# A transformer kernel on one Trainium2 core: suffix sums and strict mask of the stick-breaking heads as f32r products, the logs split in two parts

## What is computed

```
z = q k^T * scale
log_keep = where(s < t, -softplus(z), 0)
tail = cumsum(log_keep from the last key back) - log_keep
w = where(s < t, exp(log_sigmoid(z) + tail), 0)
out = w v
```

## Time and profile before

| | |
|---|---|
| median of 3 runs | 2950.47 us (2950.24 to 2952.39) |
| profiled execution, own time | 2949.88 us |
| its span | 2948.1 us, 34780 instructions |
| PE busy | 2692.4 us (91%) |
| PEld busy | 2109.6 us (72%) |
| DVE busy | 1543.8 us (52%) |
| ACT busy | 967.8 us (33%) |
| POOL busy | 333.3 us (11%) |
| mean DMA | 119 GB/s |

### The profile page before, as it was taken

One profiled execution on the slowest core, in us unless ns is written; L12 is line 12 of the kernel. 1 busy time (PEld: TensorE's weight loads), 2 busy tenths in 40 slices (PEclk: granted clock), 3 DMA queues, 4 the chain that ended last, 5 costly groups with the idle time before them and its releaser, 6 DMA issues. The chain is left out here.

```text
span 2948.1 us, 34780 instructions
## 1 busy us (share of the span) xinstructions
PE 2692.4 (91%) x14205; PEld 2109.6 (72%) x14205; DVE 1543.8 (52%) x2162; ACT 967.8 (33%) x1349; POOL 333.3 (11%) x193
## 2 busy tenths in 40 slices
PE   6899999999998999999998898999997788997975
PEld 5777688888876777888886787888775755685542
DVE  4672356544637523555544763565645488455413
ACT  3243433222322534322222332333531178430001
POOL 0000004422400000044421000000100000001110
PEclk8999999999989999999999998999998799898998
DMA  4211124443412111244443132233423120148996
GB/s 130 70 60 44 58 86 129 132 142 117 122 59 69 58 43 55 91 140 137 135 129 100 57 91 80 96 91 103 129 77 130 61 87 2 60 168 320 418 419 273
DMA packets 274792, 351.27 MB, mean 119 GB/s; under 512 B 55108, under 2 KB 251972, under 8 KB 261956
## 3 DMA queue, kind: packets, MB, share of 16 engines
q1 hardware_dynamic: 266084, 327.97, 33.1%
q0 software_dynamic: 8448, 20.98, 2.0%
q10 hardware_dynamic: 96, 0.02, 0.0%
HBM read 332.13 MB, written 25.17 MB: 121 GB/s over the span
## 5 line engine op out<-in xcount | busy, mean ns | idle before, releaser
L199 PE MATMUL ps<-h_hi,w_hi 128*128 128x512 f32 x1760 | 709.4, 403 | 60.4 <-DVE room L823 21.3
L200 PE MATMUL ps<-h_lo,w_hi 128*128 128x512 f32 x1760 | 695.6, 395 | 0.0
L201 PE MATMUL ps<-h_hi,w_lo 128*128 128x512 f32 x1760 | 695.6, 395 | 0.0
L176 ACT ACTIVATE w_hi<-w_raw 128x2048 fp32r<-128x2048 f32 (+1 forms) x170 | 322.3, 1896 | 875.2 <-PE ps L201 867.1
L181 DVE TENSOR_TENSOR w_lo<-w_raw,w_hi 128x2048 fp32r<-128x2048 f32 (+1 forms) x170 | 435.9, 2564 | 253.6 <-ACT w_hi L176 253.6
L199 PEld LDWEIGHTS ps<-h_hi,w_hi 128*128 128x128 f32 x1760 | 337.6, 192 | 144.7 <-issue 72.5
L201 PEld LDWEIGHTS ps<-h_hi,w_lo 128*128 128x128 f32 x1760 | 336.3, 191 | 72.6
L200 PEld LDWEIGHTS ps<-h_lo,w_hi 128*128 128x128 f32 x1760 | 337.6, 192 | 70.1 <-issue 1.9
L201 PE MATMUL ps<-merged_hi,w_lo 128*128 128x512 f32 x640 | 252.8, 395 | 0.0
L199 PE MATMUL ps<-merged_hi,w_hi 128*128 128x512 f32 x640 | 252.8, 395 | 0.0
L200 PE MATMUL ps<-merged_lo,w_hi 128*128 128x512 f32 x640 | 252.8, 395 | 0.0
(11 more groups left out here) (456 smaller groups left out, 3767.9 us busy)
## 6 DMA issues: line engine op xcount, KB each, us to landing
w_raw<-in_w_in SPq DMA_DIRECT2D x284, 256.0 KB, 3.7
w_raw<-in_w_up SPq DMA_DIRECT2D x128, 256.0 KB, 3.6
w_raw<-in_w_down SPq DMA_DIRECT2D x128, 256.0 KB, 3.6
room<-in_w_ada SPq DMA_DIRECT2D x96, 256.0 KB, 5.9
expert_over_h<-in_w_exp_down SPq DMA_DIRECT2D x10, 1024.0 KB, 26.0
w_raw<-in_w_out SPq DMA_DIRECT2D x32, 256.0 KB, 3.5
spilled<-projected POOLq DMA_DIRECT2D x32, 256.0 KB, 2.5
w_raw<-in_w_ssm_out SPq DMA_DIRECT2D x32, 256.0 KB, 3.6
```

Source lines behind the costliest of these rows:

```text
L176: act.activation(self.hi[:, q, :, 0:cols], raw[:, q, :, 0:cols], ACT.Copy).then_inc(self.hi_ready, 1)
L199: pe.matmul(out, w[0], x[0], start=start, stop=False)
L200: pe.matmul(out, w[0], x[1], start=False, stop=False)
L201: return pe.matmul(out, w[1], x[0], start=False, stop=stop)
```

## The change

The suffix sums and the mask become f32r matmuls. The four constants (identity, strict mask, triangle, all ones) are rounded once at the start of each layer by ACT. The output of `softplus` is rounded by ACT (`split_high`) and the remainder taken by DVE (`split_low`); each of the 10 products of a head is made twice, with the high and with the low part. `suffix_sums` waits for `sp_low`, `logs(h)` of the next pair waits for `sp_low` in place of `r_ready`, and the wait for `ob_ready` moves from `weights` to `split_high`. The buffers of the stage are laid out anew: the two parts take the place of `room_w`, `swa_p` and `swv`, and `w` is in the room of the high part.

```diff
+            ident_r, strict_r, suffix_r, ones_r = (in_halves(n, [P, P]) for n in ("ident_r", "strict_r", "neg_suffix_r", "neg_ones_r"))
...
+            sp_hi, sp_lo = in_halves("sp_hi", [P, 2, PACK]), in_halves("sp_lo", [P, 2, PACK])
...
                 def scores(i):
                     if i == 0:
+                        pe.wait_ge(rounded, 4)
...
-                            mm = pe.matmul(z_ps(h)[:, SOFF[b]:SOFF[b] + P], self.c("ident"), self.c("strict"), start=False, stop=True, skip_group_check=True)
+                            mm = pe.matmul(z_ps(h)[:, SOFF[b]:SOFF[b] + P], ident_r[:], strict_r[:], start=False, stop=True, skip_group_check=True)
...
                 def suffix_sums(h):
-                    pe.wait_ge(sp_ready, h + 1)
+                    pe.wait_ge(sp_low, h + 1)
                     for b in range(TB):
                         for j in range(b, TB):
                             a = SOFF[b] + P * (j - b)
-                            mm = pe.matmul(z_ps(h)[:, a:a + STRIP[j]], self.c("neg_suffix") if j == b else self.c("neg_ones"),
-                                           sp_[:, h % 2, SOFF[j]:SOFF[j] + STRIP[j]], start=False, stop=j == TB - 1, skip_group_check=True)
+                            for part in (sp_hi, sp_lo):
+                                mm = pe.matmul(z_ps(h)[:, a:a + STRIP[j]], suffix_r[:] if j == b else ones_r[:], part[:, h % 2, SOFF[j]:SOFF[j] + STRIP[j]],
+                                               start=False, stop=j == TB - 1, skip_group_check=True)
                     mm.then_inc(r_ready, 1)
...
                 def logs(h):
                     act.wait_ge(z_ready, h + 1)
                     if h >= 2:
-                        act.wait_ge(r_ready, h - 1)
+                        act.wait_ge(sp_low, h - 1)
...
+                def split_high(h):
+                    act.wait_ge(sp_ready, h + 1)
+                    if h >= 2:
+                        act.wait_ge(ob_ready, h // 2)
+                    act.activation(sp_hi[:, h % 2], sp_[:, h % 2], ACT.Copy).then_inc(sp_high, 1)
+
                 def weights(h):
                     act.wait_ge(r_ready, h + 1)
-                    if h >= 2:
-                        act.wait_ge(ob_ready, h // 2)
...
+                for to, name in ((ident_r, "ident"), (strict_r, "strict"), (suffix_r, "neg_suffix"), (ones_r, "neg_ones")):
+                    act.activation(to[:], self.c(name), ACT.Copy).then_inc(rounded, 1)
...
                 logs(0)
                 logs(1)
                 for i in range(SBH // 2):
+                    split_high(2 * i)
+                    split_high(2 * i + 1)
                     if i >= 1:
                         take_values(i - 1)
...
+                def split_low(h):
+                    dve.wait_ge(sp_high, h + 1)
+                    dve.tensor_tensor(sp_lo[:, h % 2], sp_[:, h % 2], sp_hi[:, h % 2].bitcast(F32), ALU.subtract).then_inc(sp_low, 1)
...
                 softplus(0)
                 softplus(1)
                 for i in range(SBH // 2):
+                    split_low(2 * i)
+                    split_low(2 * i + 1)
                     for t in beside(i):
                         dense(t)
```

More of the change, by code:

```diff
@@ L493, in mix @@
                 "z_ready", "absd", "z_expd", "logd", "sp_ready", "r_ready", "w_ready", "ob_ready", "ob_taken"))
-            room = sb("mix_room", [P, 4 * PACK])
-            swv, v = sb("swv", [P, TB, SWK]), sb("v", [P, TB, SBW])
-            p = sb("swa_p", [P, 2, TB, BAND])
+            sp_high, sp_low, rounded = sem("sp_high"), sem("sp_low"), sem("rounded")
+            v = sb("v", [P, TB, SBW])
             mx, neg, den, sink, inv = (sb(f"swa_{x}", [P, 2, TB]) for x in ("mx", "neg", "den", "sink", "inv"))
@@ L499, in mix @@
             x_rs, t_rs = sb("x_rs", [P, S]), sb("token_rs", [P, TB])
-            part = lambda a, n: room[:, a * S:(a + n) * S].rearrange("p (n s) -> p n s", s=S)
-            sq, rs, tc, ts = part(0, 2), part(2, 4), part(6, 2), part(8, 2)
+            in_halves = lambda n, shape: st.enter_context(nc.sbuf_tensor(f"{n}_{l}", shape, F32R))
+            ident_r, strict_r, suffix_r, ones_r = (in_halves(n, [P, P]) for n in ("ident_r", "strict_r", "neg_suffix_r", "neg_ones_r"))
+            until_band = st.enter_context(ExitStack())
+            at_first = lambda n, shape: until_band.enter_context(nc.sbuf_tensor(f"{n}_{l}", shape, F32))
+            room = sb("mix_room", [P, 2 * PACK])
+            room_w, p, swv = at_first("mix_room_w", [P, 2 * PACK]), at_first("swa_p", [P, 2, TB, BAND]), at_first("swv", [P, TB, SWK])
+            until_band.close()
+            sp_hi, sp_lo = in_halves("sp_hi", [P, 2, PACK]), in_halves("sp_lo", [P, 2, PACK])
+            chunks_of = lambda a, n: a.rearrange("p (n s) -> p n s", s=S)[:, 0:n]
+            tc = chunks_of(room_w[:, 0:4 * S], 4)[:, 0:2]
+            rs, sq = chunks_of(room[:, 0:4 * S], 4), chunks_of(room_w[:, 2 * S:4 * S], 2)
+            ts = p[:].rearrange("p i b n -> p (i b n)").rearrange("p (n s) -> p n s", s=S)[:, 0:2]
             pt = room[:, 0:2 * len(turns) * P].rearrange("p (i n) -> p i n", i=2)
-            sp_, w = (room[:, i * 2 * PACK:(i + 1) * 2 * PACK].rearrange("p (i n) -> p i n", i=2) for i in range(2))
+            sp_, w = (a[:].rearrange("p (i n) -> p i n", i=2) for a in (room, room_w))
             x = self.swq
```

## The result

The changed kernel took 2957.86 us (median of 10 runs, 2953.98 to 2962.26), the kernel before in the same session 2951.10 (10 runs, 2949.36 to 2953.45): a ratio of 1.0021, with a 95% interval from 1.0012 to 1.0031. It is 6.8 us slower; the prediction called a change slower from 0.2% on, and the interval has this bound inside it, so the two are not told apart. The profiled execution took 2956.63 us with a span of 2954.8, against 2949.88 and 2948.1 before.

What follows compares the result with a forecast made beforehand. The PE, never idle in the stick-breaking stage, was taken as the bound. Pairs -7.2, short-stall clock falls +5.1 and first-pair falls +4.4 gave +2.3 us: about 2952.5 us for the median, range 2944 to 2960.

Steps and rivals of the forecast that it cites:

- The PE's saving: Stick-breaking stage: suffix sums 2.76 us a head against 4.25, mask 0.90 us a pair; 32 us if nothing else changed.
- The chain from z to the suffix sums: ACT and DVE list orders delay a pair's first suffix sums until 11.23 us after its first mask matmul.
- The stalls: New PE waits on `split_low` before suffix sums: 4.8 us in two first pairs, 2.4 in six others.
- A pair: Two heads in the stage: 30.45 us, against 29.47 in 2 pairs and 31.97 in 6; -7.2 us in all.
- The clock: PE clock falls after stalls: 3 of 6 short ones, +5.1 us; both first pairs at 2.2 us each, +4.4.
- The stages in all: Both layers' stick-breaking stages together: -7.2 + 5.1 + 4.4 = +2.3 us.
- Rival (a): The clock holds in the short stalls: -2.8 us, 2947.7; chance 0.20.
- rival (b): The clock falls in every pair, and for longer: 2957 to 2965 us, slower; chance 0.16.
- (c): No stall before the suffix sums, splits being ready earlier; the PE's saving counts whole: 2918.4 us; chance 0.05.
- (d): The f32r matmuls get no quicker: 4.25 us more a head, 68 us in all; chance 0.02.
- No DMA is moved: Claim about the stage that the change shifts no DMA transfer; no time was added for it.
- what stays hidden: Stage work claimed off the critical path: second head's splits, half-tile take (0.7 us cover left), `take_values`, `ob_ready`, constant roundings.

Runs made afterwards that it cites:

- the filler run: The changed kernel plus 36 unread f32r matmuls ahead of the first pair's wait for `split_low`: 2950.26 us, ratio 0.9995 to the kernel before.

## Why the prediction was right in the stage and short outside it

The time lies within the range, 5.4 us above the forecast, and 1.5 us past the 2956.4 from which it would be called slower (a chance of 0.23, against 0.61 for no change). The range was wide enough for an error that it did not foresee: the stages came out 2.0 us below the forecast, and some 6 us came on top elsewhere.

- **The PE's saving.** Right: 2.73 us a head for the forecast 2.76, the mask 0.95 and 1.04 for 0.90. That the head fits so well is partly luck, since two paces miss in opposite directions: the eight matmuls of 128 columns take 0.74 us for 0.90, the four of 384 take 0.76 for 0.69. The whole saving is given back, since the start of the suffix sums is set by ACT and DVE.
- **The chain from z to the suffix sums.** Right: 244.97 - 234.41 = 10.56 us for the forecast 10.57 + 0.10. The stalls show as 4.61 and 2.19 us for 4.7 and 2.3, eight of them, and the two list orders are shown as their cause by the runs without splits (-30.0 us in the stages) and with interleaved splits (no wait left in six of the eight pairs).
- **A pair.** 30.29 us at full clock, forecast 30.45. Without the clock a layer is 3 x 1.68 - 0.82 = 4.2 us shorter, 8.4 in all (forecast 7.2).
- **The clock.** Right in kind. The first pairs lost 32.98 - 30.29 = 2.7 us and some 2.9 (forecast 2.2 each), which the filler run shows to be clock. Of the six short stalls two were followed by a fall, 31.85 - 30.29 = 1.56 us each (forecast three at 1.7). The windows of the changed kernel that begin with the second and the third pair's stall of layer 0:

```profile
275.77:283.00 7.23, 5.04 (x24) 4.77 (x24) 6.46 (x5) 4.39 (x5) 0.00 (x0) 0.76 0.01 2
307.62:315.00 7.38, 5.20 (x31) 4.68 (x32) 4.16 (x4) 3.36 (x4) 0.00 (x0) 1.00 0.00 0
```

  The same idle of 2.19 us, once 0.76 and once 1.00. In all 8.7 us for the forecast 9.5. The Trainium skill, page "TensorE: Matmul & The Clock Gate", section "Why this matters for your kernels", warns of longer idles only; here these falls came behind 2.19 us, so its warning does not reach far enough.
- **The stages in all:** +0.3 us for +2.3. Rival (a), the clock holding, and rival (b), a fall in each pair, are both excluded by the six short stalls; (c) by the waits; (d) by 2.73 us a head.
- **The step that failed** is a term that the sum did not have. "No DMA is moved" and the list of what stays hidden priced each added instruction in its own stage. That 16 more instructions in DVE's program could lengthen the idle at a branch some 1800 us after the last of them was not thought of, though the 10.3 us of idle with nothing to wait for stood in the trace of before. It cost 6 us, more than all the errors of the terms that were there.

## What to carry to other kernels

Before an operand that the critical engine waits for is split into passes on other engines, write down those engines' lists: the passes belong right behind their producer, not behind the neighbour's work. Here this order decided between 0 and 28 us, and the faster suffix sums were worth nothing without it. When a kernel with branches moves by a few us, look at the idle ahead of a branch's target in both traces, and try the kernel before with as many instructions that never run, before the difference is put down to the edit.

## What was not expected of the hardware

- The place of an engine's instructions around a taken branch costs up to 6 us: DVE's idle ahead of the last stage was 10.1 to 10.5 us in five builds with the 160 instructions or without the 16 (before among them), and 15.7 to 16.6 in seven others, with nothing between. The count of `split_low` alone does not decide it: the kernel without splits has none and yet has the long gap of 15.9 us.
- Two f32r matmuls in series on the same 128x128 stationary operand: the second one of 128 columns on all ones starts after 0.05 to 0.06 us, not 0.112 (257.14 - 257.08, beside the 0.11 of 257.25 - 257.14, in the changed kernel's timeline). It is so in three of a head's four such pairs; in the fourth, on the triangle, it is 0.11 (258.51 to 258.62). Of 384 columns one takes 0.18 us (256.66 - 256.48), of the 0.173 taken.

```profile
256.48 0.34 PE L652 MATMUL ps<-sp_hi,neg_ones_r 128*128 128x384 f32 x1
256.66 0.34 PE L652 MATMUL ps<-sp_lo,neg_ones_r 128*128 128x384 f32 x1
...
257.08 0.23 PE L652 MATMUL ps<-sp_hi,neg_ones_r 128*128 128x128 f32 x1
257.14 0.27 PE L652 MATMUL ps<-sp_lo,neg_ones_r 128*128 128x128 f32 x1
257.25 0.39 PE L652 MATMUL ps<-sp_hi,neg_suffix_r 128*128 128x384 f32 x1
```

- The clock's falls behind short idles are not chance from one execution to the next: the changed kernel and those with 64 and with 160 more instructions lost it at the same two pairs of six. With a wait of 1.74 us it never fell, with 2.19 it fell twice in six, with the 2.33 of the interleaved kernels all four times, and work put into an earlier idle moved the fall to another pair.
